# A transformer step with an indexer, retention and 384 expert gathers: fillers of the opening, tile 1's scores, tile 2's top-132 and two queries moved

## The reference, cut to what matters

```python
def layer(x, ...):
    h = rmsnorm(x, ln1_g)
    q_a, k_a, v_a, q_i, k_i, w_i, q_b, k_b, v_b, g_b = project(h, w_in)
    # indexer: score[t, s] = sum_h w_i[t, h] * relu(q_i[t, h] . k_i[s]); the top 64 keys (tiles 0, 1)
    # or 132 of 528 keys (tile 2) take part in the attention
    o_a = dsa(q_a, q_i, w_i, k_a, v_a, k_i)
    o_b = retention(q_b, k_b, v_b, g_b)
    x = x + concat(o_a, o_b) @ w_out
    h2 = rmsnorm(x, ln2_g)
    q = (h2 @ w_query)                      # 8 heads, 2 halves of 128
    # per head: top 16 of 128 scores of each half, top 16 of their 256 sums -> e_idx (16 experts of 16384)
    u = exp_u[e_idx]                        # the gather: 8 heads x 16 = 128 rows for each token
    act = gelu(u . h2)
    x = x + sum((gate * act) * exp_v[e_idx])
    return rmsnorm(x, ln_final_g)
```

## Time and profile before

| | |
|---|---|
| time, median of 3 runs | 1145.78 us (1145.49 to 1146.57) |
| time of the profiled execution | 1147.66 us |
| its span, first to last instruction | 1145.9 us |
| bytes moved by DMA | 456.58 MB, mean 398 GB/s |
| of them the gathers | 402.68 MB |
| PE busy | 865.3 us (76%) |
| DVE busy | 786.2 us (69%) |
| POOL, ACT busy | 536.6 us (47%), 453.6 us (40%) |
| first gather issued | 109.91 us |

### The profile page before, as it was taken

The page is one execution under the profiler, slowest core; times in us unless marked ns, Lnnn a source line. Parts: engine busy times, 40 slices in busy tenths (PEclk is TensorE's granted clock), DMA queues, the critical chain, the costliest instruction groups (busy, mean ns, idle before and its releaser), DMA issues.

```text
span 1145.9 us, 12084 instructions
## 1 busy us (share of the span) xinstructions
PE 865.3 (76%) x3884; PEld 400.4 (35%) x3884; DVE 786.2 (69%) x2005; ACT 453.6 (40%) x1423; POOL 536.6 (47%) x437
## 2 busy tenths in 40 slices
PE   8999988997896867685677787577667757655555
PEld 6748743443232424242233342133223222211111
DVE  2325877876677789986676776757777767667554
ACT  2121453433444344542554663343433333333334
POOL 0002544553555455563453553555564655565442
PEclk9999999999999789897897999899897788887779
DMA  9902999999999999999999999999999999999996
GB/s 376 408 2 71 419 424 426 426 426 430 424 427 426 426 419 426 397 391 414 425 428 424 425 426 429 405 426 428 425 427 427 426 427 426 428 425 428 427 427 271
DMA packets 66790, 456.58 MB, mean 398 GB/s; under 512 B 8227, under 2 KB 10019, under 8 KB 15526
## 3 DMA queue, kind: packets, MB, share of 16 engines
q0 software_dynamic: 55888, 402.68, 83.8%
q1 hardware_dynamic: 10694, 52.87, 11.4%
q10 hardware_dynamic: 144, 0.26, 0.1%
HBM read 451.49 MB, written 3.24 MB: 397 GB/s over the span
## 4 chain that ended last, share of the span: by engine, by line
DMA 49%; PE 25%; DVE 10%; POOL 7%; ACT 5%; issue 4%; SPq 0%; POOLq 0%; DVEq 0%
DMA rows<-in_uv,ids 37%; PE ps L598 25%; DMA wt<-in_uv,ids 9%; DVE rows L2042 5%; POOL rows L537 3%; POOL work L520 2%; ACT wt L1249 2%; ACT work L1249 1%; DMA wt<-in_uv,last_ids 1%; DMA rows<-in_w_qi 1%; ACT wgt L1249 1%; DMA wt<-in_w_q 1%; DVE wt L2042 1%; POOL wt L537 1%; PE ps L601 1%
## 5 line engine op out<-in xcount | busy, mean ns | idle before, releaser
L537 POOL DMA_INDIRECT rows<-in_uv,ids x352 | 399.2, 1134 | 445.6 <-PE ps L598 361.8
L598 PE MATMUL ps<-rows,work 128*64 128x512 f32 x1416 | 412.0, 711 | 241.3 <-ACT work L1249 238.3
L2042 DVE CUSTOM_DVE_ANT_0 rows<-rows,wt 128x1024 f32<-128x1024 f32 x226 | 276.9, 1225 | 159.9 <-DMA rows<-in_uv,ids 154.1
L1249 ACT ACTIVATE zact<-zdot 128x1 f32<-128x1 f32 x354 | 71.4, 202 | 487.9 <-DVE zdot L2042 477.2
L598 PEld LDWEIGHTS ps<-rows,work 128*64 128x64 f32 x1416 | 96.6, 152 | 474.0 <-ACT work L1249 327.1
L598 PE MATMUL ps<-wt 128*128 128x128 f32 (+6 forms) x724 | 197.2, 477 | 27.0 <-ACT wt L1249 24.9
L2042 DVE CUSTOM_DVE_ANT_0 rows<-rows,masks 128x1024 f32<-128x1024 f32 x128 | 157.6, 1233 | 68.7 <-DMA rows<-in_uv,ids 66.8
L598 PEld LDWEIGHTS ps<-wt 128*128 128x128 f32 (+2 forms) x724 | 99.0, 188 | 106.0 <-issue 60.4
L1249 ACT ACTIVATE work<-pair,wgt 128x64 f32<-128x64 f32 x354 | 123.1, 348 | 11.5
L1249 ACT ACTIVATE wgt<-zact,gates 128x1 f32<-128x1 f32 x354 | 104.3, 295 | 11.5
L598 PEld LDWEIGHTS ps<-work,wt 128*128 128x128 f32 (+1 forms) x664 | 85.6, 204 | 50.3 <-issue 49.8
(11 more groups left out here) (178 smaller groups left out, 726.4 us busy)
## 6 DMA issues: line engine op xcount, KB each, us to landing
wt<-in_w_q SPq DMA_DIRECT2D x7, 2048.0 KB, 15.7
rows<-in_uv,ids POOLq DMA_INDIRECT x352
rows<-in_w_out SPq DMA_DIRECT2D x2, 2048.0 KB, 32.1
wt<-in_w_out SPq DMA_DIRECT2D x2, 2048.0 KB, 11.9
wt<-in_ckv SPq DMA_DIRECT2D x16, 256.0 KB
x<-in_x SPq DMA_DIRECT2D x5, 512.0 KB, 8.8
rows<-in_w_qi SPq DMA_DIRECT2D x1, 2048.0 KB, 13.5
wt<-in_w_qa SPq DMA_DIRECT2D x1, 2048.0 KB, 12.4
```

Of the source, the lines that this page charges most:

```text
L537: pool.indirect_dma_start(row[s], None, a["uv"], bass.IndirectOffsetOnAxis(ap=ids[:, own(n // KP).start + n % KP:own(n // KP).start + n % ...
L598: return nc.tensor.matmul(out, lhsT, rhs, start=start, stop=stop)
L1249: return nc.scalar.activation(*args, **kw)
L2042: V.tensor_tensor_reduce(row[s][:, 0:D], row[s][:, 0:D], h2r[t][:, n % 2, :], 1.0, 0.0, ALU.mult, ALU.add, zdots[s]).then_inc(dotted, 1)
```

## The change

Five edits. (1) `index_queries` counts single products instead of groups of 8, and the opening has 3, 4, 2 and 23 of tile 1's (was 8, 8, 8, 8) and then 4 of tile 2's (was 8) between the steps that lead to the first gather; the transposes of h2 are split in two halves, each behind its half of h2, and the wait for the sum of squares, which writes where h2T will stand, moves from PE to ACT and DVE; `spread_out(0)` goes behind `sums_1(0)` instead of `sums_1(1)`. (2) `y_start(0)` leaves the opening for tick 12; `add_experts(0)` opens the sum instead. (3) `scores_1(0)` moves from tick 0 to tick 6, `scores_1(1)` from tick 6 to tick 8. (4) On DVE half of tile 1's eight rounds, and its bias, are done behind picks 0 to 4 instead of ahead of pick 0. (5) Tile 2's rounds take two ticks each; rounds 0 to 8 run at ticks 93 to 110, 9 to 14 at 129 to 140, 15 and 16 at 145 to 148. The queries of units 11 and 12 are hurried and begin at ticks 136 and 148 (were 128 and 144).

```diff
-        AHEAD, HURRIED, FAST = (1, 2, 15, 16), (2, 3, 7, 8, 16), (2, 3, 16, 17, 18)
+        AHEAD, HURRIED, FAST = (1, 2, 15, 16), (2, 3, 7, 8, 11, 12, 16), (2, 3, 16, 17, 18)
         def q_at(u):
-            return {2: 8, 3: 10, 4: 20, 7: 72, 8: 88, 16: 224, 17: 230}.get(u, 16 * u - 48)
+            return {2: 8, 3: 10, 4: 20, 7: 72, 8: 88, 11: 136, 12: 148, 16: 224, 17: 230}.get(u, 16 * u - 48)
...
+            def h2_t0(e):
+                pe.wait_ge(gained, e + 1)
+                for c in range(4 * e, 4 * e + 4):
+                    last = tr(ps[:, 3 * e, (c % 4) * P:(c % 4 + 1) * P], h2[:, c * P:(c + 1) * P])
+                if e:
+                    last.then_inc(h2t_ps, 1)
...
             mm(ps[:, 2, 0:P], e8[64:64 + HI, :], kiw[64:64 + HI, P:2 * P]).then_inc(w_ps, 1)
-            index_queries(1, 6, 0, 1)
-            h2_t(0)
-            index_queries(1, 6, 1, 2)
+            h2_t0(0)
+            index_queries(1, 6, 0, 3)
+            h2_t0(1)
+            index_queries(1, 6, 3, 7)
             query(0)
-            index_queries(1, 6, 2, 3)
+            index_queries(1, 6, 7, 9)
             query_scores(0)
-            index_queries(1, 6, 3, 4)
+            index_queries(1, 6, 9, 32)
             pe.wait_ge(gb_sb, 1)
-            index_queries(2, 7, 0, 1)
+            index_queries(2, 7, 0, 4)
...
             sums_1(0)
+            spread_out(0)
             dots_1(3)
             sums_1(1)
-            spread_out(0)
             sums_1(2)
             sums_1(3)
-            index_queries(2, 7, 1, 4)
+            index_queries(2, 7, 4, 32)
             query(1)
             later_qa(0)
             query_scores(1)
             pe.wait_ge(qi_sb, 3)
-            y_start(0)
             add_experts(0)
...
             def attention_1():               # PE
+                yield from until(6)
                 scores_1(0)
-                yield from until(6)
+                yield from until(8)
                 scores_1(1)
+                yield from until(12)
+                y_start(0)
                 yield from until(14)
...
             def h2_take(t):                  # ACT and DVE
                 act.wait_ge(h2t_ps, t + 1)
+                if t == 0:
+                    act.wait_ge(sqd, H2_STAT[0] + 1)
...
-            for r in range(0, TOPK[1], 8):
+            for r in range(0, TOPK[1] // 2, 8):
                 whole(score_round(score1, r, TOPK[1], 0))
                 whole(score_round(score1, r, TOPK[1], 1))
-            set_bias(bias1, score1)
...
             def attention_1():               # DVE
+                for r in range(TOPK[1] // 2, TOPK[1], 8):
+                    whole(score_round(score1, r, TOPK[1], 0))
+                    yield from score_round(score1, r, TOPK[1], 1)
+                set_bias(bias1, score1)
                 yield from until(8)
...
                 for r in range(0, TOPK[2], 8):
-                    yield
-                    if r % 32 == 24:
-                        yield
+                    if r == 72:
+                        yield from until(129)
+                    if r == 120:
+                        yield from until(145)
                     for part in range(2):
                         yield from score_round(score2, r, TOPK[2], part)
```

More of the change, by code:

```diff
@@ L628, in keys_values, with index_queries @@
                 natural(t, w_kv, 6 + t % 2, NKV).then_inc(kv_ps, 1)
[L630 to L635, removed]
+            def index_queries(t, bank, i0, i1):
+                for i in range(i0, i1):
+                    j, c = divmod(i, KC)
+                    last = mm(ps[:, bank, j * P:(j + 1) * P], w_qi[:, c, j * P:(j + 1) * P], hT(t, c), c == 0, c == KC - 1)
+                if i1 == 4 * KC:
                     last.then_inc(qi_ps, 1)
@@ L646, in _ @@
             pe.wait_ge(w_in["qi"], 16)
-            index_queries(0, 4, 0, 2)
+            index_queries(0, 4, 0, 16)
             norm_t(1)
-            index_queries(0, 4, 2, 3)
+            index_queries(0, 4, 16, 24)
             norm_t(2)
-            index_queries(0, 4, 3, 4)
+            index_queries(0, 4, 24, 32)
             keys_values(1)
@@ L787, in scores_1 @@
                 last.then_inc(sc_ps, 1)
-            def h2_t(t):
[L790 to L794, removed]
+            def h2_t0(e):
[4 more added lines that the diff above has]
+                    last.then_inc(h2t_ps, 1)
+            def h2_t(t):
+                pe.wait_ge(hready, TILES + t + 1)
                 if t == 1:
@@ L866, in y_start @@
                 for e in range(2):
-                    last = mm(ps[:, Y_BANK[t] + e, :], ident[:], x[:, t, e * 512:(e + 1) * 512], True, False)
+                    last = mm(ps[:, Y_BANK[t] + e, :], ident[:], x[:, t, e * 512:(e + 1) * 512], t > 0, False)
                 last.then_inc(y_init, 1)
@@ L880, in add_experts @@
                         s = ring(n + j)[0]
-                        last = mm(ps[64 * j:64 * j + 64, Y_BANK[n // (HP * KP)] + e, :], diag[s], row[s][:, D + e * 512:D + (e + 1) * 512], False, stop)
+                        last = mm(ps[64 * j:64 * j + 64, Y_BANK[n // (HP * KP)] + e, :], diag[s], row[s][:, D + e * 512:D + (e + 1) * 512], n == 0, stop)
                 last.then_inc(acc, 1)
@@ L1718, in h2_take @@
                 dve.wait_ge(h2t_ps, t + 1)
+                if t == 0:
+                    dve.wait_ge(sqd, H2_STAT[0] + 1)
                 if t > 0:
```

## The result

| | before | changed |
|---|---|---|
| median of 4 runs each, same chip | 1145.91 us | 1152.55 us (1152.05 to 1154.34) |
| span of the profiled execution | 1145.9 us | 1151.0 us |
| ratio | | 1.0062, 95% interval 1.0049 to 1.0074 |

Slower by 6.6 us; forecast were 4.3 us, 1150.1, with 1142.8 to 1155.0 as the range. The medians divided give 1.0058, where the recorded ratio is 1.0062, or 7.1 us; from the experiments on, the recorded ratios are compared.

A forecast was written before the change was run, and what follows sets the result against it. DMA bytes were taken to bound the kernel from the first gather on. Opening and scores +6.4 and later picks -2.1 gave +4.3 us, 1150.1 us on the median; own range 1148 to 1152.5, with rivals 1142.8 to 1155.0.

The forecast's parts named there:

- 3.1 + 3.6 + 0.5 = +7.2: DMA holes before gathers 18 and 20, 3.1 and 3.6 us, plus 0.5 us for restarting from an empty queue.
- -2.1 + 1.3 - 2.1 = -2.9: First gather 2.1 us earlier, a 1.3 us hole behind the first twelve gathers, and 2.1 us won at later picks.
- Opening, gain and its hole: Up to block 1: first gather at 107.8, -2.1 us; PE's pairs and block 1 only 0.6 earlier, hole +1.3 us.
- The chain of the scores: Tile 1's late scores, with query(2) ahead of scores_1(1), delay pairs 10 and 12, gathers 18 and 20: holes 3.1 and 3.6 us.
- the later part, "-2.1 us": Tile 2's moved rounds and units 11 and 12: DMA holes at later picks shrink, -2.1 us, from -4.0 to +5.5.
- The +1.0 for dense rounds at picks 98 to 112: Nine instead of six of tile 2's rounds at picks 93 to 110 cost +1.0 us (bounds 0 and +2.5).
- rival 3: Later holes move with tile 2's rounds: 0 instead of -2.1 us, total 1152.2; chance 0.17.
- I take nothing for it: PE's lower clock, 1.2 GHz, after 3 us pauses before pairs 8 and 10: counted as zero in the sum.
- rival 2: Pauses before pairs 8 and 10 put PE on 1.2 GHz; second hole 3 to 4.5 us larger, 1154; chance 0.15.
- The first byte: POOL's gathers flow about 1.8 us after issue by the trace, where the Trainium skill gives about 1 us.

The follow-up runs named there:

- e2: Changed kernel with scores_1(0) and scores_1(1) back at ticks 0 and 6, all else of the change kept; 1144.16 us, ratio 0.9994 to the kernel before.
- e12: The same program as e2 run once more; 1144.33 us, ratio 0.9994 to the kernel before.
- e5: Changed kernel with 16 unused bf16 products on PE ahead of pair 8 and 16 ahead of pair 10; 1150.38 us, ratio 1.0042 to the kernel before.
- e3: Kernel before with only the new opening: single-product fillers, split transposes, spread_out(0) behind sums_1(0); 1145.16 us, ratio 1.0004.
- e4: Kernel before with only tile 2's rounds and the queries of units 11 and 12 moved; 1144.62 us, ratio 1.0001.
- e6: Changed kernel with both scores_1(0) and scores_1(1) at tick 6, ahead of pair 8 and query(2); 1145.02 us, ratio 1.0002 to the kernel before.
- e9: Changed kernel with y_start(0) right behind scores_1(1) at tick 8 instead of tick 12; 1148.91 us, ratio 1.0030 to the kernel before.
- e10: Changed kernel with scores_1(0), scores_1(1) and y_start(0), in this order, all at tick 6; 1143.51 us, ratio 0.9986 to the kernel before.
- e11: e10 with tile 2's rounds and the queries of units 11 and 12 as in the kernel before; 1143.73 us, ratio 0.9986 to the kernel before.
- e8: Kernel before, unchanged, profiled a second time; span of the profiled execution 1142.8 us.
- e1: Kernel before with only tile 1's scores moved, to ticks 6 and 8; 1149.23 us, ratio 1.0041.
- e7: e2 with add_experts(4) between later_qa(2) and later_qa(3) instead of behind both; 1150.49 us, ratio 1.0051 to the kernel before.

## Why the prediction was right in sign and short in size

By the medians' ratios (0.1% is 1.15 us), e2 and e12 part the change in two:

| part | predicted | measured |
|---|---|---|
| scores late and block 2 held behind dmask (picks 12 to 26) | 3.1 + 3.6 + 0.5 = +7.2, the clock at nothing | +7.8 (1.0062 against 0.9994), of it the clock about 2.3 (e5) |
| everything else | -2.1 + 1.3 - 2.1 = -2.9 | -0.7 (0.9994), from -1.7 to +0.3 |
| sum | +4.3 | +7.1 |

Edits 2 and 4 have no run of their own; edits 1 and 5 alone (e3, e4) give +0.5 and +0.1.

**Opening, gain and its hole: right in kind.** The start gained more (2.9 for 2.1), as spread_out(0) went at 105.99 and not near 106.8, and picks 0 to 12 lost about 1.6 for 1.3, as the argument has it: PE's pairs and block 1 don't move along with the gathers. They moved more than I had, though: block 1 went at 138.64, 1.7 us earlier and not 0.6. That the hole came out near 1.3 is in part luck, two terms that were each too small by about 1 us. e3 shows the mechanism by itself, 2.7 won and 3.3 lost.

**The chain of the scores: the right links in the right order, with two sizes off that partly cancel.** Pair 8 went at 148.36 (149.6), since pair 6, at 140.96, had its diagonal 1.1 us before the 142.1 that I gave; then pair 8 and query(2) at the lower clock took 8.1 us to the scores, not 5.7. So came scores_1(1) at 156.45 (155.3), pair 10 at 161.78 (160.6), pair 12 at 170.52 (169.1), gather 18 at 165.75 (162.8), block 2 at 174.78 (173.3). Gather 18 is later than the chain alone has it, 4.0 us behind its pair and not 2.2, because the pair itself ran at the lower clock. e6 shows that the place behind pair 8 and query(2) is the cause; e9, with block 2 at 168.52, speaks for the hold behind dmask as a second one, with the clock not parted from it. Without the clock this part is 7.8 - 2.3 = 5.5 us (e5 against e2, roughly 3.4 to 7.6), so that my 7.2 may have been somewhat too much, with what I left out to cover it. The changed kernel's own profile has 9.6 us at these picks, more than the medians give.

**The step that failed: the later part, "-2.1 us".** In the trace the stretches have 425, 416 and 426 GB/s where the earlier trace rows has 410, 358 and 363. By picks, the first and the third hole closed (0.1 for 0.7 us at picks 98 to 106, none for 2.5 at 137 to 144), while the second only shrank, 1.2 for 1.9 us at picks 123 to 129: the changed kernel is some 5 us later there, and part of it stands at 474 to 498 (411 GB/s). The +1.0 for dense rounds at picks 98 to 112 was wrong, as they cost nothing. Yet in the medians edit 5 gives 0 (e4; e10 against e11). That is the total of rival 3, but not in this profile its mechanism; e4 and e5 do lose 1.0 and 1.1 us at picks 129 to 137, where the other kernels with edit 5 lose 0.1. Two things in the profiles speak to it, though neither was changed by itself: the earlier trace rows came from an execution 3.1 us longer than the next one (e8), with 5.2 us of loss at picks 98 to 144 where the other has 3.4; and beside the new opening 1.9 us come back at picks 160 to 240 (e10 against e11), which I had no term for. The second doesn't explain e4, which loses 1.0 us there. These 2.1 us are most of the miss of 2.8 by the ratios; the split has an uncertainty of 1 to 2 us.

**The second: "I take nothing for it", the clock.** It was rival 2, with 0.15, and its mark came in, if a little ahead of the 149 to 157 that I gave: the clock was at 0.50 from 148 to 152. The price is about 2.3 us, not 3 to 4.5. The ground for leaving it out, shorter pauses at the full clock in the records of before, was none: I had myself forecast pauses longer than the 2.48 us of the earlier trace rows.

**The first byte.** From 107 to 112 us the changed kernel shows

```profile
107.00:108.00 1.00, 1.00 (x6) 0.62 (x5) 0.00 (x0) 0.00 (x0) 1.00 (x1) 1.00 0.00 0
108.00:109.00 1.00, 1.00 (x6) 0.88 (x5) 0.00 (x0) 0.38 (x1) 0.69 (x2) 1.00 0.30 57
109.00:110.00 1.00, 1.00 (x5) 0.68 (x4) 0.00 (x0) 0.21 (x1) 0.69 (x2) 1.00 0.85 197
```

With the gather issued at 107.00, 57 GB/s are 0.13 us of full rate before 109, so the flow began near 108.9, 1.9 us behind the issue, as in the earlier trace rows. The Trainium skill (DMA: Bandwidth & Descriptors, Specifications) has about 1 us on this path; here too the trace disagrees.

## What to carry to other kernels

Where an engine runs a fixed list, a small step that others wait for belongs ahead of a long one whose result nobody needs yet: two products with a chain behind them, put behind a pair and a 16-product query, cost some 5 to 8 us, and moving them ahead of both recovered it (e6). Before an earlier start is counted as a gain, ask what comes when the first full queue is used up; if that is set by an engine without a pause, the gain is lost there. When a change opens pauses on TensorE that are longer than any in the old trace, price the lower clock; and credit no gain of 2 us to holes that only one profile shows.

## What the runs showed of the hardware

All five pauses of 3.67 us on PE, in the changed kernel, e1 and e9, were followed by the lower clock (a pair 3.68 us for 1.94), and so was one of 3.26 us in e7. The pause before pair 12 lasts 2.47 to 2.49 us in ten profiles. In three of them, e2 and e6, the clock stayed up; in seven it fell (e3 and e10, two pairs in 5.35 us for 3.65; e7, 3.60 for one; e4, e8, e11 and e12). It fell behind pauses of 2.2 us as well (before pair 12 in e5 and e9). Two programs were profiled twice: e2 and e12, shown above, and the kernel before, where the earlier trace rows has two pairs in 3.65 us and e8 has

```profile
161.55 5.15 PE L598 MATMUL ps<-rows,work 128*64 128x512 f32 x16 [2.49 <-ACT work L1249]
```

So for the same program and a pause of the same length the clock falls in one execution and not in the next; what decides stays open here. A single profile therefore doesn't tell whether a pause of 2.5 us is free. In e8 the lower clock cost nothing (no loss at picks 12 to 26), in e12, where dmask and block 2 stood behind the slow pair, some 1.5 us went with it.

And the same program, profiled twice, had spans of 1145.9 and 1142.8 us, 1.8 of the 3.1 us in DMA holes at picks 98 to 144.
